# Norms moved beside matmuls in a two-block transformer forward: group norms, feed-forward norm, router weights, zero fill

## The chip, the cores and the metric

One core of a Trainium2 chip runs one program. The metric is the device time of one execution in microseconds (us), lower is better. Engines: TensorE (PE in the rows, its weight loads PEld), VectorE (DVE), ScalarE (ACT), GpSimd (POOL) and SyncE (SP), which here only issues DMAs and waits. A name with a q (SPq, PEq) is the engine's sequencer.

## The reference, cut to what matters

Two blocks of a network in fp32, on 512 tokens (and 256 context tokens in the first block) of width 1024. The change touches only the second block:

```
def second_block(x, ...):
    mod = silu(c) @ w_mod + b_mod             # six vectors: shift, scale, gate for mixer (m) and feed-forward (f)
    h = rms_norm(x, norm_mix) * (1 + scale_m) + shift_m
    proj = h @ w_in                           # 16 tiles of 128 columns (+ 4 columns for the forget gates)
    y_a = sliding_window_sink_attention(...)  # 512 columns, tiles 0..3
    y_b = rg_lru(conv(x_b)) * gelu(g_b)       # 256 columns, tiles 4, 5
    y_c = forgetting_attention(...)           # 256 columns, tiles 6, 7
    y = concat([rms_normalize(y_a), rms_normalize(y_b), rms_normalize(y_c)]) * out_gain
    x = x + gate_m * (y @ w_out)
    h = rms_norm(x, norm_ffn) * (1 + scale_f) + shift_f
    # router: 4 groups, 4 experts in each; best group by h @ w_rg, its best 2 experts by h @ w_re
    # each chosen expert: (silu(h @ w_gate[e]) * (h @ w_up[e])) @ w_down[e], weighted and summed
    x = x + gate_f * hierarchical_moe(h, ...)
    return rms_norm(x, norm_final)
```

## The kernel before, in words

**Layout.** Activations lie feature-major: `x` is [128, 8, 768], feature 128 k + p of a token in partition p of tile k. A matmul in near fp32 precision is three fp32r matmuls: every operand is split into a high part (rounded to fp32r, by ScalarE) and a low part (operand minus high part, by VectorE), and hi*hi, lo*hi and hi*lo are summed in PSUM (lines 912 to 914). Plain fp32 matmuls (the sums of squares against a matrix of ones, the transposes) take two passes each, and each pass is a record of its own.

**Blocks.** The program is a sequence of `nc.Block()`s. In a block each engine has a queue of its own, written out by hand in program order, tied by semaphores (`Tally`: a semaphore and the value it has reached). At a block's end all engines meet at a barrier. Semaphore waits stop the whole queue of the waiting engine.

**run_dense** (line 814) is the block for dense layers. A layer is cut into pieces of 128 output columns; each piece is one weight load of 512 KB on SP's queue (line 885) into one of two buffers, the split of the weights (ScalarE line 924, VectorE line 934), 24 matmuls of 512 columns (8 tiles times three) into one of two PSUM places, and the output by ScalarE or VectorE. The queue of ScalarE and of VectorE is, for piece n: split of piece n+1, then `behind` (a background program's step n), then the output of piece n. On TensorE step n of the background stands ahead of piece n. With `norm=` a norm runs in the same block: its sums come first, then the splits of pieces 0 and 1, then its apply part; TensorE waits tile by tile in piece 0 (`first_use`).

**Norms.** `normalize` (line 448) is a block of its own: squares on ScalarE (487), fp32 sums against ones on TensorE (476, in which two squares are ahead at most), variance on VectorE (525), Sqrt on ScalarE (489), reciprocal on VectorE (527), then per tile a multiplication (539) and gain on ScalarE (500), with `post` also high and low parts for the next matmuls (494, 547, 532). `Norm` is the same for use inside another block; in it POOL does the multiplication of the odd tiles (674) and VectorE that of the even ones, the high part is ScalarE's (614), the low part VectorE's (661, 665). With `xn=` the product goes to two scratch tiles, so POOL's tile k waits for the low part of tile k-2.

**The second block before.** (1) `run_dense` with the mixer's `Norm`, 16 pieces of `w_in_2` in the order `Branches.ORDER`, and `Branches` as background: convolution, LRU gates and scan, forget-gate cumulative sums, GELU, transposed values. Its last VectorE steps are those of n = 11 (1995 to 1999); the LRU's output is `xc`. POOL's program for the block (`Branches.pool`) ends with a memset and a DMA on POOL's queue, which writes zeros to all of `y_rows`, the experts' output rows in DRAM (2032 to 2034), and a wait for it. (2) `Branches.attend`: 24 units of two heads each through `Heads`; the output tiles end in `proj` 0 to 3 and 6, 7 (line 1314). SP does nothing there. (3) Three `normalize` blocks for y_a (4 tiles), y_b (2) and y_c (2), in place or into `proj`. (4) `run_dense` with the 8 pieces of `w_out_2`, ahead of which `split_before` splits all eight tiles of y (1064, 1069); TensorE waits for all eight. VectorE adds each piece to `x` (995). (5) `prenorm`: a `normalize` block for the feed-forward norm, 8 tiles, with `post`. (6) `experts`, one block to the end.

**experts.** SP loads the router's weights and some constants, then the experts' weights into five buffers of 1 MB (`e_raw`; a refill waits for the low part of the piece that lay there). The router has tokens as the stationary operand: for each of 4 groups of 128 tokens 8 x 3 matmuls with 20 moving columns (2394 to 2396). Then 64 matmuls against the identity turn h to token-major rows (2405, 2406), ScalarE copies them out (2501) and POOL stores them to DRAM (2353). VectorE meanwhile does some 60 small dependent instructions of the routing (2165 to 2231); in between TensorE sums the choices (2414, 2416). POOL scatters the slots (2357), reads them back, and gathers the rows of the first of 23 blocks of 128 tokens (2372), on which TensorE waits (2431). The blocks of experts follow, with a final norm at the end.

## Time and profile before

Three runs: 3625.29, 3631.13, 3632.75 us, median 3631.13. The profiled execution took 3634.53 us; its span from first to last instruction is 3632.5, mean granted TensorE clock 0.911 of 2.4 GHz.

| engine | busy us | share | instructions |
|---|---|---|---|
| PE | 3075.6 | 85% | 15929 |
| DVE | 1739.5 | 48% | 2638 |
| ACT | 1200.6 | 33% | 1833 |
| POOL | 488.1 | 13% | 419 |

DMA moved 338.73 MB, on average 93 GB/s. The second block takes the last 712 us of the span, from 2920 on. A timeline row reads: start in us from the span's start, duration (of a merged group: from its first start to its last end), engine, line, operation, output<-input, shapes, how many, and in brackets the idle time before it with what ended it. A row of `--windows` form gives a stretch, its length, busy time and count for PE, PEld, DVE, ACT and POOL, then granted clock, DMA share and GB/s.

### The profile page before, as it was taken

Reading aid. Unit: us, or ns where it says so; the run is one execution under the profiler, and the core shown is the slowest. Engines: PE = TensorE matmul, PEld = TensorE weight load, DVE = VectorE, ACT = ScalarE, POOL = GpSimd, SP = SyncE. Lnnn points to the kernel's source line nnn. Section 1 sums busy time; section 2 is a strip of 40 time slices with the busy share of each in tenths; the row PEclk is TensorE's granted clock in tenths of the full one; section 3 lists DMA queues with packets and bytes.
Section 4 is the critical chain, followed back from the end, with each engine's and each line's share of the span. In section 5 each row is a group of like instructions: output and inputs, shape, how many; then the busy total and the mean of one; then the engine's idle time right before and its main releaser. Section 6 shows DMA issues by size and latency. Waiting matters only on the chain. (4 is left out here: it accounts for less than half of the span.)

```text
span 3632.5 us, 39858 instructions
## 1 busy us (share of the span) xinstructions
PE 3075.6 (85%) x15929; PEld 2429.6 (67%) x15929; DVE 1739.5 (48%) x2638; ACT 1200.6 (33%) x1833; POOL 488.1 (13%) x419
## 2 busy tenths in 40 slices
PE   5579869799987999999698688997999977766995
PEld 3468545588875888888485456775878745346774
DVE  3664365422235554553512653335555352643886
ACT  4222344421113221221323453223222233522774
POOL 2240112200011000001311131001000003202222
PEclk8689989999997999999799899998999978885997
DMA  4774010122211443331440103322656226014971
GB/s 155 154 147 124 8 21 1 43 62 54 58 41 51 120 124 102 116 111 41 69 83 25 21 1 81 91 72 86 184 156 181 65 52 187 1 47 144 326 255 70
DMA packets 424353, 338.73 MB, mean 93 GB/s; under 512 B 38043, under 2 KB 372937, under 8 KB 424041
## 3 DMA queue, kind: packets, MB, share of 16 engines
...
## 5 line engine op out<-in xcount | busy, mean ns | idle before, releaser
L912 PE MATMUL ps<-ahi,w_hi 128*128 128x512 f32 (+1 forms) x2384 | 870.7, 365 | 171.6 <-DVE alo L665 84.0
L914 PE MATMUL ps<-alo,w_hi 128*128 128x512 f32 (+1 forms) x2384 | 858.2, 360 | 0.0
L913 PE MATMUL ps<-ahi,w_lo 128*128 128x512 f32 (+1 forms) x2384 | 857.9, 360 | 0.0
L912 PEld LDWEIGHTS ps<-ahi,w_hi 128*128 128x128 f32 x2384 | 462.0, 194 | 258.5 <-issue 60.0
L934 DVE TENSOR_TENSOR w_lo<-w_raw,w_hi 128x1024 fp32r<-128x1024 f32 (+2 forms) x248 | 359.8, 1452 | 445.0 <-ACT w_hi L924 444.2
L914 PEld LDWEIGHTS ps<-alo,w_hi 128*128 128x128 f32 x2384 | 461.5, 194 | 68.3
L913 PEld LDWEIGHTS ps<-ahi,w_lo 128*128 128x128 f32 x2384 | 462.6, 194 | 64.1
L924 ACT CAST w_hi<-w_raw 128x1024 fp32r<-128x1024 f32 (+2 forms) x248 | 289.5, 1169 | 507.4 <-PE ps L914 351.2
L746 DVE SCALAR_TENSOR_TENSOR vec_acc<-vec_w,csilu,vec_acc 128x512 f32<-128x512 f32 x364 | 263.0, 768 | 24.5 <-DMA vec_w<-in_w_mod 20.3
L1378 POOL TENSOR_SCALAR prob<-prob,nm 128x512 f32<-128x512 f32 (+4 forms) x104 | 163.8, 1575 | 717.8 <-DVE nm L1303 717.8
L1010 POOL TENSOR_TENSOR xsum<-x 128x768 f32<-128x768 f32 (+1 forms) x4 | 7.2, 1800 | 1485.9 <-DVE x L995 1485.9
L912 PE MATMUL ps<-hhi,w_hi 128*128 128x512 f32 (+1 forms) x528 | 190.6, 361 | 10.1 <-DVE hlo L1043 10.1
L995 DVE SCALAR_TENSOR_TENSOR x<-ps,mod,x 128x512 f32<-128x512 f32 x80 | 51.5, 669 | 289.4 <-PE ps L914 289.4
L913 PE MATMUL ps<-hhi,w_lo 128*128 128x512 f32 (+1 forms) x528 | 189.2, 358 | 0.0
L914 PE MATMUL ps<-hlo,w_hi 128*128 128x512 f32 (+1 forms) x528 | 188.7, 357 | 0.0
L1087 ACT ACTIVATE sg<-ps 128x768 f32<-128x768 f32 (+1 forms) x48 | 33.8, 705 | 425.4 <-PE ps L914 425.4
L1346 ACT ACTIVATE prob<-ps,nm 128x512 f32<-128x512 f32 (+4 forms) x208 | 140.4, 675 | 98.2 <-DVE nm L1296 58.4
L1248 PE MATMUL ps<-ident,prob 128*128 128x128 f32 x800 | 128.0, 290 | 30.9 <-ACT probT L1356 25.3
L1356 ACT COPY probT<-ps 128x384 f32<-128x384 f32 (+3 forms) x272 | 121.7, 477 | 81.2 <-PE ps L1248 81.1
L1095 DVE TENSOR_TENSOR gp<-sg,ps 128x768 f32<-128x768 f32 (+1 forms) x32 | 26.3, 821 | 244.0 <-ACT sg L1087 244.0
L2496 ACT CAST e_hi<-e_raw 128x2048 fp32r<-128x2048 f32 x69 | 131.5, 1911 | 29.4 <-DMA e_raw<-in_w_up 15.7
L1248 PEld LDWEIGHTS ps<-ident,prob 128*128 128x128 f32 x800 | 87.9, 145 | 76.8 <-issue 51.0
...
## 6 DMA issues: line engine op xcount, KB each, us to landing
vec_w<-in_w_mod SPq DMA_DIRECT2D x128, 512.0 KB, 4.2
...
```

What stands on the lines that cost most here:

```text
L746: m = dve.scalar_tensor_tensor(out=acc, in0=w, scalar=f, in1=acc, op0=ALU.mult, op1=ALU.add)
L912: pe.matmul(o, whi[:, j, b0 + b, :], hi[:, b, t0:t0 + tn], start=(b == 0), stop=False)
L913: pe.matmul(o, wlo[:, j, b0 + b, :], hi[:, b, t0:t0 + tn], start=False, stop=False)
L914: m = pe.matmul(o, whi[:, j, b0 + b, :], lo[:, b, t0:t0 + tn], start=False, stop=(b == nb - 1))
L924: act.copy(whi[:, j, 0:d.blocks, :], raw[:, j, 0:d.blocks, :]).then_inc(hi_ready[j].sem, 1)
L934: dve.tensor_tensor(wlo[:, j, 0:d.blocks, :], raw[:, j, 0:d.blocks, :], whi[:, j, 0:d.blocks, :].bitcast(F32), ALU.subtract).then_inc(lo_r ...
L995: m = dve.scalar_tensor_tensor(out=xo, in0=ps[:, b + t0:b + t0 + tn], scalar=mod[:, v, bass.ds(i * 2 + (gate + jj), 1)], in1=xo, op0=ALU.m ...
L1248: m = pe.transpose(ps[:, o:o + P], self.prob[:, j, n % self.bufs, (b0 + b) * P:(b0 + b + 1) * P], ident[:])
L1346: act.activation(self.prob[:, j, slot, 0:u.keys], self.scores_of(n, j), ACT.Exp, bias=nm[:, j, slot, 0:1], scale=self.sign, accum_out=nm[: ...
L1356: act.copy(self.probT[:, j, n % 2, b0 * P:(b0 + nb) * P], ps[:, o:o + nb * P]).then_inc(pt_done.sem, 1)
L1378: pool.tensor_scalar(self.prob[:, j, slot, 0:u.keys], self.prob[:, j, slot, 0:u.keys], self.nm[:, j, slot, 3:4], None, ALU.mult).then_inc( ...
L2496: act.copy(whi[:, n % HI, :], raw[:, n % RAW, :]).then_inc(e_hi.sem, 1)
```

## The change

- **Zero fill.** The memset and the DMA that writes zeros to `y_rows` leave `Branches.pool`. In the attention block POOL clears a tile of its own (`y_zero`) ahead of its work, and SP issues the DMA on its queue and waits for it there.
- **y_b.** Its norm is done by background steps in the input projection: squares on ScalarE at n = 12, two sums on TensorE ahead of piece 14, variance at n = 14, Sqrt, reciprocal and two multiplications in place at n = 15.
- **y_a and y_c.** A new class `GroupNorm` is the `norm=` of the output projection. It does six tiles of sums, two variances, two reciprocals; POOL multiplies tiles 1, 3 and 7, VectorE 0, 2 and 6. The gain is applied while the high and low parts are made, also for y_b, so `split_before` is gone.
- **Feed-forward norm.** `prenorm`'s block is gone. `experts` makes a `Norm` with scratch in `tok_major` and runs it inside its block, with the parts of each engine behind the first small steps of that engine.
- **Router.** The router's weights (20 columns) are the stationary operand and 512 tokens move: 8 x 3 matmuls, each tile's when its low part is there. ScalarE copies the [20, 512] logits to `lgT`, TensorE turns them in four transposes behind the first eight of the 64 row matmuls, and VectorE reads them from another bank.

```diff
+        class GroupNorm:
+
+
+            def __init__(self, c, proj, y_b, hi, lo):
+                self.y = [proj[:, k, :] for k in range(4)] + [y_b[:, k, :] for k in range(2)] + [proj[:, 6 + k, :] for k in range(2)]
+                self.hi, self.lo = hi, lo
+                self.sq = [sb(c, f"gr_sq{n}", [P, LAT])[:] for n in range(2)]
+                self.rstd = [sb(c, f"gr_rstd{n}", [P, LAT])[:] for n in range(2)]
+                self.stats = [(0, k) for k in range(4)] + [(1, k) for k in (6, 7)]
+
+                self.every = dict(zip((norm_sq, norm_var, norm_c, norm_sqrt, norm_rstd, *norm_x2, norm_hi, norm_lo), (6, 6, 2, 2, 2, 3, 3, KT, KT)))
+                self.c0 = {t: t.base for t in self.every}
+
+            def sem(self, t, n):
+                return t.sem, self.c0[t] + n
+
+            def total(self, gi):
+                return ps[:, BANK * (1 + gi):BANK * (2 + gi)]
+
+            def gain(self, k):
+                return col(vec3, V3_GAIN + k)
+
+            def act_stats(self, act):
+                for m, (gi, k) in enumerate(self.stats):
+                    if m >= 2:
+                        act.wait_ge(*self.sem(norm_var, m - 1))
+                    act.activation(self.sq[m % 2], self.y[k], ACT.Square).then_inc(norm_sq.sem, 1)
+
+            def pe(self, pe):
+                for m, (gi, k) in enumerate(self.stats):
+                    pe.wait_ge(*self.sem(norm_sq, m + 1))
+                    pe.matmul(self.total(gi), ones[:], self.sq[m % 2], start=(k in (0, 6)), stop=(k in (3, 7))).then_inc(norm_var.sem, 1)
+
+            def first_use(self, pe, k):
+                pe.wait_ge(*self.sem(norm_lo, k + 1))
+
+            def dve_stats(self, dve):
+                for gi, upto in ((0, 4), (1, 6)):
+                    dve.wait_ge(*self.sem(norm_var, upto))
+                    dve.tensor_scalar(self.rstd[gi], self.total(gi), 1.0 / (P * (4, 2)[gi]), RMS_EPS, ALU.mult, ALU.add).then_inc(norm_c.sem, 1)
+
+            def act_apply(self, act):
+                for gi in range(2):
+                    act.wait_ge(*self.sem(norm_c, gi + 1))
+                    act.activation(self.rstd[gi], self.rstd[gi], ACT.Sqrt).then_inc(norm_sqrt.sem, 1)
+                for k in range(KT):
+                    if k in (1, 3, 7):
+                        act.wait_ge(*self.sem(norm_x2[1], (k + 1) // 2 - (k == 7)))
+                    if k in (0, 2, 6):
+                        act.wait_ge(*self.sem(norm_x2[0], k // 2 + 1 - (k == 6)))
+                    act.activation(self.hi[:, k, :], self.y[k], ACT.Identity, scale=self.gain(k)).then_inc(norm_hi.sem, 1)
+
+            def dve_apply(self, dve):
+                def inverse(gi):
+                    dve.wait_ge(*self.sem(norm_sqrt, gi + 1))
+                    dve.reciprocal(self.rstd[gi], self.rstd[gi]).then_inc(norm_rstd.sem, 1)
+                    dve.wait_ge(*self.sem(norm_rstd, gi + 1))
+
+                def even(k, gi):
+                    dve.tensor_tensor(self.y[k], self.y[k], self.rstd[gi], ALU.mult).then_inc(norm_x2[0].sem, 1)
+
+                def low(k):
+                    dve.wait_ge(*self.sem(norm_hi, k + 1))
+                    dve.scalar_tensor_tensor(out=self.lo[:, k, :], in0=self.y[k], scalar=self.gain(k), in1=self.hi[:, k, :].bitcast(F32),
+                                             op0=ALU.mult, op1=ALU.subtract).then_inc(norm_lo.sem, 1)
+
+                inverse(0)
+                even(0, 0)
+                even(2, 0)
+                low(0)
+                low(1)
+                inverse(1)
+                even(6, 1)
+                for k in range(2, KT):
+                    low(k)
+
+            def pool(self, pool):
+                for m, (k, gi) in enumerate(((1, 0), (3, 0), (7, 1))):
+                    pool.wait_ge(*self.sem(norm_rstd, gi + 1))
+                    pool.tensor_tensor(self.y[k], self.y[k], self.rstd[gi], ALU.mult).then_inc(norm_x2[1].sem, 1)
+
+            def ended(self):
+                for t, n in self.every.items():
+                    t.base += n
...
+                if n == 14:
+                    pe.wait_ge(yb_square.sem, 2)
+                    for k in range(2):
+                        m = pe.matmul(ps[:, 6 * BANK:6 * BANK + LAT], ones[:], self.tmp[:, k, :], start=(k == 0), stop=(k == 1))
+                    m.then_inc(yb_sum.sem, 1)
...
+                    act.wait_ge(yb_done.sem, 1)
+                    for k in range(2):
+                        act.activation(self.tmp[:, k, :], self.xc[:, k, :], ACT.Square).then_inc(yb_square.sem, 1)
+                if n == 15:
+                    act.wait_ge(yb_var.sem, 1)
+                    act.activation(self.r[:, 0, :], self.r[:, 0, :], ACT.Sqrt).then_inc(yb_root.sem, 1)
...
-                    ch.mark(dve.tensor_tensor(self.xc[:], self.xc[:], self.r[:], ALU.mult))
+                    dve.tensor_tensor(self.xc[:], self.xc[:], self.r[:], ALU.mult).then_inc(yb_done.sem, 1)
                     dve.wait_ge(swa_in.sem, 32)
                     ch.mark(dve.tensor_scalar(self.nsinks[:], self.sinks[:], -1.0, None, ALU.mult))
+                if n == 14:
+                    dve.wait_ge(yb_done.sem, 1)
+                    dve.wait_ge(yb_sum.sem, 1)
+                    dve.tensor_scalar(self.r[:, 0, :], ps[:, 6 * BANK:6 * BANK + LAT], 1.0 / LRU_W, RMS_EPS, ALU.mult, ALU.add).then_inc(yb_var.sem, 1)
+                if n == 15:
+                    dve.wait_ge(yb_root.sem, 1)
+                    ch.link(dve.reciprocal(self.r[:, 0, :], self.r[:, 0, :]))
+                    for k in range(2):
+                        ch.mark(dve.tensor_tensor(self.xc[:, k, :], self.xc[:, k, :], self.r[:, 0, :], ALU.mult))
...
-                zero = self.ck[:, 0:2, :].rearrange("p a n -> p (a n)")
-                pool.memset(zero, 0.0).then_inc(pool_chain.sem, 1)
-                pool.wait_ge(pool_chain.sem, p + 1)
-                pool.dma_start(y_rows[:].rearrange("(r b) d -> r b d", b=N_BLOCKS), zero.unsqueeze(1).to_broadcast([P, N_BLOCKS, D])).then_inc(y_zeroed.sem, 16)
-                pool.wait_ge(y_zeroed.sem, 16)
...
-                attend(Heads(c, units))
+                zero = sb(c, "y_zero", [P, D])
+                z0 = pool_chain.base + 1
+
+                def cleared(pool):
+                    pool.memset(zero[:], 0.0).then_inc(pool_chain.sem, 1)
+
+                def fill(sp):
+                    sp.wait_ge(pool_chain.sem, z0)
+                    sp.dma_start(y_rows[:].rearrange("(r b) d -> r b d", b=N_BLOCKS), zero[:].unsqueeze(1).to_broadcast([P, N_BLOCKS, D])).then_inc(y_zeroed.sem, 16)
+                    sp.wait_ge(y_zeroed.sem, 16)
+
+                attend(Heads(c, units, before={"pool": cleared}), fill)
+                pool_chain.base += 1
...
+            spare = tm[:].rearrange("p t d -> p (t d)").rearrange("p (n m) -> p n m", m=LAT)
+            norm = Norm(c, xt(LAT), LAT, RMS_EPS, lambda k: col(vec1, V_FFN + k), (ahi, alo, *modulate_by(mod, 3)),
+                        [spare[:, 0, :], spare[:, 1, :]], spare[:, 2, :], [spare[:, 3, :], spare[:, 4, :]], xn=[spare[:, 5, :], spare[:, 6, :]])
+            lgT = spare[0:NG + N_EXP, 7, :]
...
+                norm.dve_stats(dve)
...
+                norm.dve_apply(dve)
                 dve.wait_ge(ld[1].sem, ld[1].base + 48)
-                dve.wait_ge(pe_chain.sem, pc + 1)
+                dve.wait_ge(t_done.sem, t_done.base + 1)
                 NR = NG + N_EXP
-                ch.link(dve.tensor_tensor(logits[:], ps[:, 7 * BANK:7 * BANK + 4 * NR].rearrange("p (t n) -> p t n", n=NR),
+                ch.link(dve.tensor_tensor(logits[:], ps[:, 5 * BANK:5 * BANK + 4 * NR].rearrange("p (t n) -> p t n", n=NR),
...
+                norm.pool(pool)
...
+                norm.pe(pe)
                 pe.wait_ge(dve_chain.sem, dc + 1)
-                for t in range(4):
-                    tok = slice(t * P, (t + 1) * P)
-                    o = ps[:, 7 * BANK + t * NR:7 * BANK + (t + 1) * NR]
-                    for k in range(KT):
-                        pe.matmul(o, ahi[:, k, tok], nw_hi[:, k, :], start=(k == 0), stop=False)
-                        pe.matmul(o, alo[:, k, tok], nw_hi[:, k, :], start=False, stop=False)
-                        m = pe.matmul(o, ahi[:, k, tok], nw_lo[:, k, :], start=False, stop=(k == KT - 1))
-                m.then_inc(pe_chain.sem, 1)
-                pe.wait_ge(act_chain.sem, ac + 2)
-                for u in range(8):
+                o = ps[0:NR, 7 * BANK:7 * BANK + LAT]
+                for k in range(KT):
+                    norm.first_use(pe, k)
+                    pe.matmul(o, nw_hi[:, k, :], ahi[:, k, :], start=(k == 0), stop=False)
+                    pe.matmul(o, nw_hi[:, k, :], alo[:, k, :], start=False, stop=False)
+                    m = pe.matmul(o, nw_lo[:, k, :], ahi[:, k, :], start=False, stop=(k == KT - 1))
+                m.then_inc(prep_mm.sem, 1)
+
+                def rows_of_h(u):
                     t, half = u // 2, u % 2
                     if u >= 4:
                         pe.wait_ge(tok_major.sem, u - 3)
@@ -2405,6 +2525,15 @@
                         pe.matmul(o, ahi[:, 4 * half + k, t * P:(t + 1) * P], ident_r[:], start=True, stop=False)
                         m = pe.matmul(o, alo[:, 4 * half + k, t * P:(t + 1) * P], ident_r[:], start=False, stop=True)
                     m.then_inc(x_turned.sem, 1)
+
+                pe.wait_ge(act_chain.sem, ac + 2)
+                rows_of_h(0)
+                pe.wait_ge(prep_act.sem, prep_act.base + 1)
+                for t in range(4):
+                    m = pe.transpose(ps[:, 5 * BANK + t * NR:5 * BANK + (t + 1) * NR], lgT[:, t * P:(t + 1) * P], ident[0:NR, 0:NR])
+                m.then_inc(t_done.sem, 1)
+                for u in range(1, 8):
+                    rows_of_h(u)
...
+                norm.act_stats(act)
+                norm.act_apply(act)
+                act.wait_ge(prep_mm.sem, prep_mm.base + 1)
+                act.copy(lgT, ps[0:NG + N_EXP, 7 * BANK:7 * BANK + LAT]).then_inc(prep_act.sem, 1)
...
-                def prenorm(v, s):
-                    with ExitStack() as c1:
-                        h = sb(c1, "h", [P, KT, LAT])
-                        normalize([h[:, k, :] for k in range(KT)], LAT, RMS_EPS, lambda k: col(vec1, v + k), post=(ahi, alo, *modulate_by(mod, s)), src=xt(LAT))
...
-                    for first, n in ((0, 4), (4, 2), (6, 2)):
-                        normalize([proj[:, first + k, :] for k in range(n)], LAT, RMS_EPS, lambda k: col(vec3, V3_GAIN + first + k),
-                                  src=[branches.xc[:, k, :] for k in range(2)] if first == 4 else None)
                     with ExitStack() as c2:
-                        run_dense(new_ring(c2, KT), [residual(mod, g["w_out_2"][0], 2 * KT, KT, (ahi, alo), LAT, adds={y_hi: KT, y_ready: KT},
-                                                              before=split_before(proj, 0, ahi, alo, KT, LAT))])
-                prenorm(V_FFN, 3)
+                        run_dense(new_ring(c2, KT), [residual(mod, g["w_out_2"][0], 2 * KT, KT, (ahi, alo), LAT)],
+                                  norm=GroupNorm(c2, proj, branches.xc, ahi, alo))
                 experts(c, ahi, alo, mod)
```

## Rows read from the trace of the kernel before

**Rows 1.** Busy times of the router's stretch (PE, PEld, DVE, ACT, POOL, clock, DMA, GB/s).
```profile
3278.00:3302.00 24.00, 20.53 (x97) 20.53 (x97) 1.58 (x13) 0.52 (x2) 2.54 (x3) 0.50 0.92 290
```

**Rows 2.** Timeline around the zero fill: start us, duration, engine, instruction, idle before.
```profile
3043.11 1.51 POOL L2034 DMA_DIRECT2D y_rows<-fox_ck  x1 [0.30 <-POOL fox_ck L2032]
3063.20 1.04 ACT L924 CAST w_hi<-w_raw 128x1024 fp32r<-128x1024 f32 x1 [7.80 <-DMA w_raw<-in_w_in]
3065.55 0.79 PE L912 MATMUL ps<-a2hi,w_hi 128*128 128x512 f32 x1 [5.19 <-DVE w_lo L934]
3086.95 0.60 ACT L970 ACTIVATE proj<-ps 128x512 f32<-128x512 f32 x1 [9.22 <-PE ps L914]
3087.86 0.93 PE L1235 MATMUL ps<-swa_k,proj 64*128 64x128 f32 x8 [0.94 <-PEq L867]
```

**Rows 3.** DMA view, 3000 to 3300 us: kilobytes, then us to landing.
```profile
y_rows<-fox_ck POOLq DMA_DIRECT2D x1, 11776.0 KB, 37.1
```

**Rows 4.** Weight buffer, landing times from 3040 to 3095, then 3010 to 3042 us.
```profile
DMA to landing us min/median/max: 6.5/16.8/25.5
DMA to landing us min/median/max: 5.7/6.4/6.5
```

**Rows 5.** Timeline at the first group norm.
```profile
3154.09 0.69 DVE L1314 COPY proj<-ps 128x512 f32<-128x512 f32 x1 [4.26 <-PE ps L1259]
3155.76 3.83 PE L476 MATMUL ps<-sq,ones 128*128 128x512 f32 x8 [1.72 <-ACT sq L487]
3158.43 1.28 ACT L489 ACT_TABLE_LOAD   x1
3161.02 3.35 DVE L527 RECIPROCAL rstd<-rstd 128x512 f32<-128x512 f32 x1 [0.69 <-ACT rstd L489]
```

**Rows 6.** Timeline of the output projection: first matmul, clock's rise, first and last update.
```profile
3202.67 0.79 PE L912 MATMUL ps<-a2hi,w_hi 128*128 128x512 f32 x1 [18.36 <-DVE a2lo L1069]
3206.68 0.55 PE L912 MATMUL ps<-a2hi,w_hi 128*128 128x512 f32 x1
3210.53 0.75 DVE L995 SCALAR_TENSOR_TENSOR x<-ps,mod,x 128x512 f32<-128x512 f32 x1 [6.78 <-PE ps L914]
3249.74 0.75 DVE L995 SCALAR_TENSOR_TENSOR x<-ps,mod,x 128x512 f32<-128x512 f32 x1 [4.85 <-PE ps L914]
```

**Rows 7.** Timeline of the mixer's norm beside its first projection tile.
```profile
2920.33 1.15 ACT L605 ACTIVATE sq<-x 128x512 f32<-128x512 f32 x2 [0.28 <-PEq L456]
2921.01 10.40 PE L592 MATMUL ps<-sq,ones 128*128 128x512 f32 x16 [12.75 <-ACT sq L605]
2933.87 0.68 DVE L646 TENSOR_SCALAR rstd<-ps 128x512 f32<-128x512 f32 x1
2938.68 1.77 POOL L674 TENSOR_TENSOR xn<-x,rstd 128x512 f32<-128x512 f32 x1 [48.02 <-DVE rstd L648]
2943.97 1.58 DVE L665 TENSOR_TENSOR a2lo<-tmp,a2hi 128x512 fp32r<-128x512 f32 x1
2954.11 0.69 DVE L665 TENSOR_TENSOR a2lo<-tmp,a2hi 128x512 fp32r<-128x512 f32 x1
2956.56 0.59 ACT L970 COPY proj<-ps 128x512 f32<-128x512 f32 x1 [2.61 <-PE ps L914]
```

**Rows 8.** Timeline, experts' block up to the routing.
```profile
3277.78 0.37 SPq L2297 DMA_DIRECT2D nw<-in_w_router_group  x1
3280.74 0.32 ACT L2508 CAST nw_hi<-nw 128x160 fp32r<-128x160 f32 x1 [3.64 <-DMA nw<-in_w_router_expert]
3301.98 0.45 PE L2405 MATMUL ps<-ident_r,a2hi 128*128 128x128 f32 x1
3308.19 0.23 DVE L2184 TENSOR_TENSOR route_both<-route_chosen 128x64 f32<-128x64 f32 x1
3315.67 4.39 PE L2414 MATMUL ps<-route_both,e_upto 128*128 128x17 f32 x20
3321.87 0.29 DVE L2199 TENSOR_TENSOR route_masked<-route_chosen,ps 128x128 f32<-128x128 f32 x1 [7.59 <-PE ps L2416]
```

5 lines of the change are left out of this document (3 added, 2 removed).

## The prediction, made before the changed kernel ran

> **What bounds the kernel now.** I read the code's order first, then the table of stretches from 3040 to 3350 us, then the timeline at each border, then the waits of the weight buffer. The program is a chain of blocks with a barrier of all engines at each end, so the chain of waits on the page begins only where the last block starts, 3277.8 us, and says nothing of the part that changes; the borders have to be read from the timeline. Four places matter.
>
> End of the input projection: 16 pieces of 24 matmuls go at 5.60 us each. The zero fill, 11,776 KB, is issued by POOL at 3043.11 and needs 37.1 us [rows 2, 3]. Weight loads issued meanwhile land after up to 25.5 us, against 5.7 to 6.5 before [rows 4]. ScalarE stands 7.80 us for a load and TensorE 5.19 us for its split; the first attention matmul is at 3087.86 [rows 2]. Group norms: attention's last copy ends at 3154.78 [rows 5] and the output projection's first matmul is at 3202.67 [rows 6], 47.9 us of three short blocks and a split in which TensorE has almost nothing. Feed-forward norm: from 3250.8, a barrier's 0.3 behind the last update's end at 3250.49 [rows 6], until the next block at 3277.78 [rows 8], TensorE again nearly empty. Router: 96 matmuls of 20 columns at half clock, 20.53 us of the stretch at 0.50 [rows 1]; the 64 transposing matmuls follow from 3301.98 to 3315.67, and the routing waited 7.59 us for what TensorE does behind them [rows 8]. So in these stages each dependent step counts in full.
>
> **Part 1, zero fill to the attention stage, LRU norm into the projection's end.** TensorE would finish piece 13 at 3065.55 - 5.19 = 3060.36 with or without the fill. Without it the loads are back at 6 us, which a piece of 5.60 us and two buffers cover (they did until 3043). Added ahead of piece 14: two fp32 sums, four passes. Eight passes took 3.83 us [rows 5], so 1.9 us; they wait for two squares that ScalarE does three pieces earlier. Everything behind them on TensorE waits too: 3060.36 + 1.9 + 2 x 5.60 = 3073.5. Then the tail on ScalarE and VectorE: Sqrt comes after ScalarE's copy of piece 14 at 3068.5, with a table load of 1.28 [rows 5] and about 0.63, so 3070.4; reciprocal 3.35 [rows 5], 3073.8; two multiplications at 0.65 to 0.69 [rows 7], 3075.1. The last copy of ScalarE is done at 3074.1, so VectorE is late last, by 1.0 us. The barrier took 3087.86 - 3087.55 = 0.3 [rows 2]: attention starts at 3075.4 instead of 3087.86, 12.5 us less. Exp's table must now be loaded again at its start; ScalarE stood there 0.9 us anyway, so 0.4 is lost. I take 12.1. Bounds: a loss of 4 (if the loads were late for another reason, the added 1.9 + 1.0 + 0.4 and slack remain), and 14.5 (sums hidden).
>
> The fill itself: POOL's memset, then one DMA on SP's queue, where nothing else is queued in that block; attention runs 3087.86 to 3154.78, 66.9 us, and the fill took 37.1. It costs nothing as long as it takes under about 65 us. No row shows this transfer on SP's queue; that queue moved 290 GB/s in 3278 to 3302 [rows 1], at which it would take 41.
>
> The Trainium skill (ScalarE: Activation LUTs, "What ACT_TABLE_LOAD costs") puts a table switch at 1.28 us and a drain of 1.38 behind it. The load in this trace is 1.28 [rows 5], and the activations that follow such loads start at once or when their operand comes. By the page the two added switches would cost up to 2.8 us more; I go by the row.
>
> **Part 2, group norms beside the output projection.** Before: 3154.78 to the end of the last update, 3249.74 + 0.75 = 3250.49 [rows 5, 6]. After, from the same point: ScalarE starts squares at 3155.1. Four tiles of sums took until 3155.76 + 3.83 = 3159.59, two per 1.85, so six until 3161.4. Weights were loaded meanwhile. ScalarE: two high halves at 1.04 [rows 2] until 3162.4, table 1.28, Sqrt, 3164.3. VectorE: two variances, then two low halves at 1.3 at most (3064.24 to 3065.55 [rows 2]) until 3164.7, reciprocal 3.35: 3168.1. Now POOL multiplies tiles 1 and 3 at 1.77 us [rows 7], VectorE tiles 0 and 2 and the low parts 0 and 1. Do they overlap? In the same kind of norm VectorE's subtraction took 1.58 instead of 0.69 when a multiplication of POOL ran [rows 7]: it stood until POOL had done. So I let them exclude each other where both want to go: low part 1 at 3172.5, second reciprocal until 3175.9, POOL's tile 7 until 3177.7, then six low parts at 0.69, the first at 3178.4. If they overlapped freely this would be 1.9 earlier. TensorE does tiles 0 and 1 alone, then six groups of three matmuls, at half clock 1.28 a group (3202.67 to 3206.68 holds nine matmuls and the clock rises there, after 4.0 us [rows 6]): three groups until 3182.4, the rest at 0.70: piece 0 is done at 3184.4. Updates come every (3249.74 - 3210.53) / 7 = 5.60 us [rows 6]: the last ends at 3184.5 + 39.2 + 0.75 = 3224.5. Gain 26.0; bounds 23.5 (the clock rises a piece's rest later, more exclusion) and 28 (free overlap).
>
> The Trainium skill (SBUF — State Buffer, "Who interferes with whom") says that a VectorE instruction with two SBUF inputs and a GpSimd instruction that reads SBUF exclude each other for the whole instruction. That speaks against giving three tiles to POOL, and the 1.58 above [rows 7] agrees; by the rule the sum is the 26.0, without it 27.9.
>
> **Part 3, feed-forward norm in the experts' block, weights of the router stationary.** Before: 3250.8 to the first transposing matmul, 3301.98 [rows 8]. After: the block starts at 3250.8, but ScalarE first waits for the router's weights: its first cast was 2.96 after that block's start (3277.78 to 3280.74 [rows 8]) and with two casts the squares start 3.5 late, 3254.3. This is a cost that the old order did not have. From there I take the mixer's norm, the same class with the same two scratch tiles, POOL on odd tiles, and TensorE cold: from the first square at 2920.33 to the last low part at 2954.11 + 0.69 = 2954.80 [rows 7]. In it VectorE did two weight splits before the variance: sums done at 2921.01 + 10.40 = 2931.41, variance at 2933.87, so 2.4 don't recur. 34.5 - 2.4 = 32.1: last low part at 3286.4. TensorE follows with three matmuls per tile, 24 instead of 96, and is 1.7 behind at the end (2954.80 to 2956.56 [rows 7]): 3288.1. The copy of the logits (some 0.6) lies beside the first eight transposing matmuls. Their four transposes are eight passes at 4.39 / 20 = 0.22 [rows 8]: 1.75. The 64 transposing matmuls stay. TensorE is thus done with them 3301.98 - 3288.1 - 1.75 = 12.1 us earlier. The routing gets its logits at 3291.6 and needs some 6.4 us to the table that TensorE multiplies (3301.98 to 3308.42 [rows 8]), 3298.0, while TensorE is at 3303.5: TensorE stays late last, the 7.59 [rows 8] shrinks little. Bounds: 9 (the norm 3 slower) and 15 (TensorE still at full clock for the sums: its gap of about 5 us is like the 5.19 after which it was at half [rows 2]).
>
> What is behind hangs on the same points: the five weight buffers of the experts fill ahead of need in both versions, and the next loads wait for VectorE, which comes out of the routing. So the 282 us behind 3350 move as a whole, at no cost.
>
> **Sum.** 12.1 + 26.0 + 12.1 = 50.2. The profiled execution took 3634.53 (span 3632.5 and 2.0 around it), so 3584.3 in its terms; it was 3.4 above the median, 3631.13, in whose terms the forecast is 3581.
>
> **Rivals.** A, *the clock rises behind the router*. The new router's 24 matmuls stream 512 columns back to back at its end, after which the mixer's clock had risen; the transposing matmuls might then run at 0.11 instead of 0.213. Against: with 64 of them in a row the clock never rose before. TensorE would be done before the routing, which would then be last at 3298.0 (5.5 less), and the 28 small matmuls behind, 3315.67 to 3321.87, would halve: about 8.5 more, 3572.5. B, *the fill was not what starved the projection*. For it: loads were 6 us, not 4, already before. Against: 25.5 right under the fill. Part 1 is then -4, total 34: 3597. C, *the group norm's two reciprocals and POOL hold TensorE longer*, with a cold clock through piece 0 and again in the norm behind: parts 2 and 3 give 23 and 7, total 42: 3589. D, *the fill on SP's queue is slow*: attention's barrier waits for it. It decides from 65 us on, and makes the kernel slower from 65 + 50 = 115 us, under 105 GB/s; at 80 GB/s it would take 147 us, 82 over: 3581 + 82 = 3663. Against: 290 GB/s on that queue [rows 1].
>
> **How the numbers follow.** Forecast 0.60, A 0.15, C 0.14, B 0.07, D 0.04. The forecast's own range is 3575 to 3587, from the parts' bounds; A and C on its sides and part of B give 3569 to 3595. A measurement tells 0.2%, 7 us, from no change. Faster by that: all but D, 0.95; within: 0.02 (a D of 110 to 120 us); slower: 0.03.
>
> **What would show it.** Part 1: in the last two pieces no wait of ScalarE on its weights; attention starts near 3075; a table load at its start; the fill lands inside attention. Part 2: 3154.78's counterpart to the last update about 70 us instead of 96, subtractions of about 1.5 us on VectorE beside POOL. Part 3: squares 3.5 us into the block, 24 router matmuls spread over the low parts, 64 transposing ones at 0.213. Wrong would be: a wait of all engines on SP at attention's end, stages behind 3350 that do not shift rigidly, or a clock of 1.0 under the transposing matmuls.

## The result and the profile after

The changed kernel takes 3585.9 us (median of 4 runs, 3578.1 to 3597.8) beside 3631.9 for the kernel before on the same chip (4 runs, 3625.3 to 3641.7): 0.9874 of it, 95% interval [0.9834, 0.9913]. Run again with the experiments it gave 3581.5, 0.9852 [0.9824, 0.9880]. The forecast was 3581. The profiled execution took 3578.06 (span 3576.3), 56.5 less than the profiled one before.

A single execution can lie 8 us off either way: the code ahead of the change is the same in every kernel here, and yet ScalarE copied piece 12 of the input projection as early as 3048.2 and as late as 3065.0 us. So I compare stretches between six borders that each trace has: that copy; attention's first matmul; the end of attention's last copy; the start of the output projection's last update; TensorE's first transpose of gathered tokens; the end of the span. All are differences of timeline rows, in us. In the labels, serial means in a block of its own, and dummies are matmuls that nothing reads.

| kernel | piece 12 at | to attention | attention | to last update | to gather | to end |
|---|---|---|---|---|---|---|
| before | 3054.80 | 33.06 | 66.92 | 94.96 | 99.74 | 283.02 |
| changed | 3052.77 | 20.49 | 66.75 | 69.29 | 85.28 | 281.72 |
| changed, again (e9) | 3060.81 | 20.49 | 66.89 | 69.42 | 85.09 | 281.80 |
| e1 fill on POOL | 3059.45 | 31.63 | 62.58 | 69.24 | 85.25 | 283.75 |
| e2 group norms serial | 3055.05 | 20.50 | 66.91 | 83.78 | 85.35 | 281.41 |
| e3 ffn norm serial | 3059.32 | 20.48 | 66.70 | 69.30 | 78.02 | 284.88 |
| e4 squares first | 3064.81 | 20.49 | 66.92 | 69.43 | 79.71 | 280.34 |
| e5 squares first, hold | 3063.10 | 20.49 | 66.97 | 69.34 | 76.49 | 280.51 |
| e6 squares first, dummies | 3053.85 | 20.49 | 62.52 | 69.46 | 71.61 | 281.67 |
| e7 group norms on VectorE | 3048.20 | 20.49 | 65.45 | 69.24 | 75.67 | 283.45 |
| e8 dummies in group norms | 3050.64 | 20.48 | 62.66 | 68.93 | 74.97 | 281.82 |
| e10 combined | 3052.18 | 20.49 | 62.49 | 66.20 | 71.95 | 281.49 |
| e11 combined, more dummies | 3064.99 | 20.49 | 65.58 | 67.78 | 73.05 | 283.01 |
| e12 ffn serial, new order | 3060.32 | 20.49 | 66.98 | 66.20 | 78.31 | 284.20 |

Of the 56.2 us between the two spans, 2.0 were there before the change begins and 1.3 come behind the gather, neither more than the same code moves from run to run. The change itself brings 12.6 in the projection's end, 0.2 in attention, 25.7 with the group norms and 14.5 with the feed-forward norm and the router: 52.9.

The timeline of the changed kernel at the projection's end and attention's start is the counterpart of [rows 2]; columns are start us, duration, engine, line, instruction, and idle time before it:

```profile
3065.68 0.60 ACT L1056 ACTIVATE proj<-ps 128x512 f32<-128x512 f32 x1 [5.78 <-PE ps L1000]
3066.30 1.28 ACT L2024 ACT_TABLE_LOAD   x1
3067.59 0.63 ACT L2024 ACTIVATE lru_r<-lru_r 128x512 f32<-128x512 f32 x1
3068.26 3.35 DVE L2103 RECIPROCAL lru_r<-lru_r 128x512 f32<-128x512 f32 x1 [6.49 <-ACT lru_r L2024]
3071.28 0.60 ACT L1056 ACTIVATE proj<-ps 128x512 f32<-128x512 f32 x1 [3.06 <-PE ps L1000]
3071.64 1.29 DVE L2105 TENSOR_TENSOR lru_x<-lru_x,lru_r 128x512 f32<-128x512 f32 x2
3073.22 1.28 ACT L1431 ACT_TABLE_LOAD   x1 [1.34 <-PEq L953]
3073.26 0.93 PE L1321 MATMUL ps<-swa_k,proj 64*128 64x128 f32 x8 [2.01 <-PEq L953]
3074.19 0.61 SPq L2176 DMA_DIRECT2D y_rows<-y_zero  x1
3074.51 0.29 ACT L1431 ACTIVATE sink_e<-swa_sinks,nm 128x1 f32<-128x1 f32 x1
```

The last two copies are 5.60 us apart and neither waits for a DMA. The copies of pieces 13 and 14 start at 3058.38 and 3065.68, 7.30 apart, since y_b's two sums stand between these pieces on TensorE. VectorE's chain on y_b ends at 3072.93, 1.05 behind ScalarE's last copy, and lets the block end. The fill goes out within attention; the DMA view from 3060 to 3120 us gives its kilobytes and the us to landing:

```profile
y_rows<-y_zero SPq DMA_DIRECT2D x1, 11776.0 KB, 33.1
```

From the timeline of the changed kernel around the output projection's first piece, VectorE, POOL and TensorE (the counterpart of [rows 5, 6]):

```profile
3139.32 0.69 DVE L1400 COPY proj<-ps 128x512 f32<-128x512 f32 x1 [5.72 <-PE ps L1345]
...
3155.04 1.71 POOL L761 TENSOR_TENSOR proj<-proj,gr_rstd 128x512 f32<-128x512 f32 x1
3155.54 2.41 DVE L745 SCALAR_TENSOR_TENSOR a2lo<-proj,vec,a2hi 128x512 fp32r<-128x512 f32 x2
3157.44 0.77 PE L998 MATMUL ps<-a2hi,w_hi 128*128 128x512 f32 x1 [10.48 <-DVE a2lo L745]
3157.88 3.34 DVE L737 RECIPROCAL gr_rstd<-gr_rstd 128x512 f32<-128x512 f32 x1
3163.67 0.79 PE L998 MATMUL ps<-a2hi,w_hi 128*128 128x512 f32 x1 [3.33 <-DVE a2lo L745]
3170.11 0.75 DVE L1081 SCALAR_TENSOR_TENSOR x<-ps,mod,x 128x512 f32<-128x512 f32 x1 [3.17 <-PE ps L1000]
...
3209.30 0.75 DVE L1081 SCALAR_TENSOR_TENSOR x<-ps,mod,x 128x512 f32<-128x512 f32 x1 [4.85 <-PE ps L1000]
```

TensorE waits twice: 10.48 us for the first low part and 3.33 for tile 2's, which stands behind the second reciprocal. Two low parts take 2.41 beside POOL. The experts' block (timeline, the counterpart of [rows 8]):

```profile
3213.72 0.32 ACT L2637 CAST nw_hi<-nw 128x160 fp32r<-128x160 f32 x1 [14.50 <-DMA nw<-in_w_router_expert]
3214.15 1.14 ACT L606 ACTIVATE tok_major<-x 128x512 f32<-128x512 f32 x2
3214.83 9.53 PE L593 MATMUL ps<-tok_major,ones 128*128 128x512 f32 x16 [5.56 <-ACT tok_major L606]
3246.68 0.31 PE L2525 MATMUL ps<-ident_r,a2hi 128*128 128x128 f32 x1
3248.41 0.61 PE L2533 MATMUL ps<-ident,tok_major 20*128 20x20 f32 x4
3249.13 0.24 DVE L2284 TENSOR_TENSOR logits<-ps,route_b 128x80 f32<-128x80 f32 x1 [3.80 <-PE ps L2533]
```

The first square waits for the cast, as forecast. Table of stretches of the same trace (busy us of PE, PEld, DVE, ACT, POOL with counts, then granted clock, DMA share, GB/s):

```profile
3233.00:3245.00 12.00, 8.87 (x20) 1.74 (x18) 11.27 (x16) 4.59 (x6) 5.13 (x4) 0.50 0.18 70
3252.00:3254.00 2.00, 2.00 (x11) 2.00 (x11) 1.69 (x10) 1.32 (x2) 0.39 (x1) 0.50 0.53 217
3268.00:3270.00 2.00, 2.00 (x11) 2.00 (x11) 1.79 (x12) 0.00 (x0) 0.00 (x0) 0.50 0.00 0
3270.00:3272.00 2.00, 2.00 (x19) 2.00 (x18) 1.76 (x16) 0.90 (x2) 0.00 (x0) 0.91 0.01 4
```

From 3233 to 3245 the router's matmuls run at the norm's pace, at 1.2 GHz (0.50). From 3246 TensorE is busy without a gap, with the 64 row matmuls and then smaller ones, and still stays at 1.2 GHz until about 3270. The experiments on the feed-forward norm turn on these rows.

### The profile page after: what moved, and what is told of

Its sections match the earlier page's. It is cut to its first block and busy times, and to the rows that moved or that the text cites. A ratio compares the mean times of both kernels' runs of the same rounds, so it can differ in the third digit from the quotient of the medians.

```text
span 3576.3 us, 39662 instructions
## 1 busy us (share of the span) xinstructions
PE 3056.3 (85%) x15861; PEld 2406.6 (67%) x15861; DVE 1741.2 (49%) x2631; ACT 1194.6 (33%) x1820; POOL 495.1 (14%) x425
## 3 DMA queue, kind: packets, MB, share of 16 engines
q1 hardware_dynamic: 409384, 307.15, 30.1%
```

## The experiments

Diffs are against the changed kernel; three dots stand for lines not shown. "Last update to gather" is the fifth column of numbers in the table above.

**e1: the fill back on POOL's queue in the input projection.**

```diff
+                zero = self.ck[:, 0:2, :].rearrange("p a n -> p (a n)")
+                pool.memset(zero, 0.0).then_inc(pool_chain.sem, 1)
+                pool.wait_ge(pool_chain.sem, p + 1)
+                pool.dma_start(y_rows[:].rearrange("(r b) d -> r b d", b=N_BLOCKS), zero.unsqueeze(1).to_broadcast([P, N_BLOCKS, D])).then_inc(y_zeroed.sem, 16)
+                pool.wait_ge(y_zeroed.sem, 16)
...
-                attend(Heads(c, units, before={"pool": cleared}), fill)
+                attend(Heads(c, units))
```

> The changed kernel with one thing undone: the zero fill of y_rows is issued on POOL's queue at the end of the input projection again, as in the kernel before; the norm of y_b stays at the projection's end. Theory: the fill is what starves the projection's last weight loads, so the wait of about 20 us for piece 14 (landing of w_raw up to 25 us) returns, and the attention stage starts about 12 us later than in the changed kernel: 3598 us beside 3586, and the norm of y_b costs nothing there, since it lies in the wait. Rival: the weights come late for another reason (the order of SP's queue) and the 12 us came from the norm of y_b alone: then the time stays within 2 us of the changed kernel and the loads land in 6 to 7 us in spite of the fill.

Measured: 3593.4 us, 0.9892 [0.9863, 0.9921]. The stretch to attention is 31.63 instead of 20.49. ScalarE's timeline shows the two waits:

```profile
3067.42 1.04 ACT L1010 CAST w_hi<-w_raw 128x1024 fp32r<-128x1024 f32 x1 [7.37 <-DMA w_raw<-in_w_in]
3080.37 1.04 ACT L1010 CAST w_hi<-w_raw 128x1024 fp32r<-128x1024 f32 x1 [11.41 <-DMA w_raw<-in_w_in]
```

Rows of the weight buffer from 3040 to 3092 us, first of e1 and then of the changed kernel (shortest, median and longest time from issue to landing):

```profile
DMA to landing us min/median/max: 6.1/17.6/25.0
```

```profile
DMA to landing us min/median/max: 6.5/6.9/7.3
```

The fill starved the projection; that is shown. Taking it out gives 11.1 us (31.63 - 20.49). Beside the fill y_b's norm costs nothing (31.63 with it, 33.06 in the kernel before without it). No run takes y_b's norm out where the fill is gone, but the rows of the changed kernel show its price there: the 7.30 us between two copies instead of 5.60, and VectorE 1.05 late at the end. In the profiled execution 4.2 us of this were given back, since attention took 62.58 instead of 66.75; that is no effect of the fill, as e6, e8 and e10 have 62.5 to 62.7 with the fill in attention. The stretches of 30 us inside attention, first e1 and then the changed kernel:

```profile
3111.00:3141.00 30.00, 25.00 (x209) 14.87 (x208) 23.39 (x112) 22.85 (x97) 12.38 (x14) 1.00 0.01 2
```

```profile
3093.00:3123.00 30.00, 25.97 (x172) 14.64 (x173) 20.91 (x100) 19.70 (x85) 10.26 (x12) 0.83 0.41 165
```

In one the clock holds, in the other it falls for some microseconds; the kernel before had 0.83 as well, with a DMA share of 0.01.

**e2: group norms ahead of the output projection, in blocks of their own** (y_b still normalized in the input projection).

```diff
+                    for first, n in ((0, 4), (6, 2)):
+                        normalize([proj[:, first + k, :] for k in range(n)], LAT, RMS_EPS, lambda k: col(vec3, V3_GAIN + first + k))
...
                     with ExitStack() as c2:
-                        run_dense(new_ring(c2, KT), [residual(mod, g["w_out_2"][0], 2 * KT, KT, (ahi, alo), LAT)],
-                                  norm=GroupNorm(c2, proj, branches.xc, ahi, alo))
+                        run_dense(new_ring(c2, KT), [residual(mod, g["w_out_2"][0], 2 * KT, KT, (ahi, alo), LAT, adds={y_hi: KT, y_ready: KT},
+                                                              before={"act": split_act, "dve": split_dve, "pe": lambda pe: pe.wait_ge(y_ready.sem, y_ready.base + KT)})])
```

`split_act` and `split_dve` (not shown) make the high and low parts of all eight tiles ahead of the projection.

> The changed kernel with the group norms taken out of the output projection again: two norms of groups 0 and 2 in blocks of their own, then the split and the projection; y_b is still normalized at the end of the input projection. Theory: what the second part gains is the serial chain of group norms and of the split, without the y_b block, so the stretch from the end of attention to the last update is 70 us plus what two of the three blocks and the split cost. In the kernel before the three norms took about 39 us of the 95.7, some 9 to 10 of them for y_b; so the stretch should be 84 to 87 us, the time about 3601 us. Rival: the overlap itself brings nothing because VectorE's and POOL's shared work sets TensorE's pace; then the stretch stays within 4 us of 70.

Measured: 3593.4 us, 0.9893 [0.9865, 0.9921]; to the last update 83.78 instead of 69.29. So the second part's 25.7 us are 14.5 from the overlap and 11.2 (94.96 - 83.78) from y_b's block, which the first part had made needless.

**e3: feed-forward norm in its own block, 24 router matmuls kept.**

```diff
-                norm.pe(pe)
                 pe.wait_ge(dve_chain.sem, dc + 1)
...
+                    normalize([h[:, k, :] for k in range(KT)], LAT, RMS_EPS, lambda k: col(vec1, V_FFN + k), post=(ahi, alo, *modulate_by(mod, 3)), src=xt(LAT))
                 experts(c, ahi, alo, mod)
```

> The changed kernel with the feed-forward norm in a block of its own ahead of the experts again; the router keeps its weights stationary (24 matmuls of 512 columns, transposes of the logits). Theory: the overlap hides the router's matmuls and the loads and casts behind the norm; serial, the norm's block takes about 31 us, then block entry, casts and the 24 matmuls (24 x 0.6 at half clock = 14 us, or 24 x 0.3 = 7 at full) run after it, so the stretch from the norm's first square to the routing's first sum grows by 8 to 14 us: 3594 to 3600 us. Rival: the gain of this part came from the 24 matmuls in place of 96 alone and the overlap is worth nothing: then within 2 us of the changed kernel.

Measured: 3580.7 us, 0.9851 [0.9825, 0.9877]. Neither theory: the gather comes 7.3 us *earlier* than in the changed kernel (78.02 against 85.28), although the logits come 1.4 later (41.23 against 39.83 behind the last update). The difference lies behind the logits. Timeline of TensorE in e3:

```profile
3251.81 0.63 PE L2508 MATMUL ps<-a2lo,nw_hi 128*20 128x512 f32 x1
3252.24 0.63 PE L2509 MATMUL ps<-a2hi,nw_lo 128*20 128x512 f32 x1
3252.66 0.53 PE L2507 MATMUL ps<-a2hi,nw_hi 128*20 128x512 f32 x1
3253.03 0.40 PE L2508 MATMUL ps<-a2lo,nw_hi 128*20 128x512 f32 x1
3253.26 0.40 PE L2509 MATMUL ps<-a2hi,nw_lo 128*20 128x512 f32 x1
```

and the stretch behind the router:

```profile
3256.00:3266.00 10.00, 10.00 (x91) 9.82 (x89) 6.30 (x40) 8.29 (x14) 2.14 (x4) 1.00 1.09 362
```

The 24 matmuls run without gaps here, the clock rises 5 us into them, and the 64 row matmuls behind start every 0.11 us instead of every 0.21. In the changed kernel the 24 come three at a time at the norm's pace and the clock stays at half. Against the kernel before, the router's new form with the norm still serial brings 21.7 us (99.74 - 78.02): 12.5 at the first row matmul (52.24 to 39.77 behind the last update), the rest behind it, where the clock is now high. In these two profiles the overlap gives 7.3 of them back. The medians can't confirm that difference, 3580.7 here and 3581.5 for the changed kernel run again.

**e4: squares ahead of the casts.** Base of e5 and e6.

```diff
+                norm.act_stats(act)
                 act.wait_ge(ld[0].sem, ld[0].base + 32)
                 act.copy(nw_hi[:], nw[:]).then_inc(act_chain.sem, 1)
                 act.copy(ident_r[:], ident[:]).then_inc(act_chain.sem, 1)
-                norm.act_stats(act)
```

> The changed kernel with one move on ScalarE in the experts' block: the squares of the feed-forward norm are issued ahead of the two casts of the router weights and of the identity, which wait for a DMA. Theory: the casts hold the first square back by 3.5 us, and the whole chain down to the routing starts at that square, so the time falls by about 3.5 us, to 3582 us (with the squares 0.5 us after the block's start). The casts then come 13 us later, still ahead of the first router matmul. Rival: the norm's first use is set by the weights' low part, which VectorE makes after the cast and ahead of its reciprocal in order; then the cast, now behind the squares, delays VectorE's variance by its own length and the gain falls to 1 to 2 us, or below nothing.

Measured: 3575.8 us, 0.9834 [0.9810, 0.9858]; the gather 79.71 behind the last update, 5.6 earlier than in the changed kernel. More than 3.5, because TensorE comes to the sums sooner behind the projection and does them at full clock:

```profile
3223.38 7.52 PE L593 MATMUL ps<-tok_major,ones 128*128 128x512 f32 x16 [1.77 <-ACT tok_major L606]
```

In the changed kernel the same group took 9.53.

**e5: e4, and TensorE waits for the last low part ahead of the router.**

```diff
+                norm.first_use(pe, KT - 1)
                 for k in range(KT):
                     norm.first_use(pe, k)
```

> Squares ahead of the casts, and TensorE waits in the experts' block for the last low part of the normed state before it starts the router's 24 matmuls, so that these run without gaps. All stretches from the last update of the output projection. With the norm serial, the logits came at 41.2 us and the gather's first transpose at 78.0, and the clock rose 5 us into the gapless matmuls, so that the 64 matmuls for the rows took 0.11 us each; with the norm beside the router (squares first) 34.5 and 79.7, with the clock at half and 0.21 us each. Theory (the clock, which the norm's pace keeps low, is what the overlap costs): the last low part is there at 30.7; 12 matmuls at 0.43 and 12 at 0.23, then the transposes: logits at about 40, gather at 77, 3 us earlier than with squares first alone in spite of the later start. Rival (the gather comes early in the serial form because loads or POOL's queue stand better there, not the clock): the logits come 5.5 us later and so does the gather, 85.

Measured: 3574.8 us, 0.9835 [0.9808, 0.9862]; logits at 39.13, gather at 76.49. The first router matmul starts 13.2 us later than in e4 (30.77 instead of 17.61 behind the last update) and the logits come 4.6 later, and yet the gather comes 3.2 earlier. That speaks for the clock and against the rival. The stretches of e5 show the clock rising among the 24, about 3 us into them:

```profile
3250.00:3252.00 2.00, 1.33 (x4) 0.54 (x5) 0.57 (x1) 0.00 (x0) 0.00 (x0) 0.50 0.02 7
3252.00:3256.00 4.00, 4.00 (x16) 1.57 (x15) 0.00 (x0) 0.00 (x0) 0.00 (x0) 0.79 0.00 0
3256.00:3260.00 4.00, 4.00 (x30) 3.06 (x29) 0.83 (x5) 1.16 (x2) 0.00 (x0) 1.00 0.00 0
```

**e6: e4, and matmuls that nothing reads while TensorE waits for the norm.**

```diff
                 for k in range(KT):
+                    for _ in range(1 if k else 7):
+                        pe.matmul(warm_bank, ones[:], x[:, 0, 0:LAT], start=True, stop=True)
                     norm.first_use(pe, k)
```

> Squares ahead of the casts, and matmuls that nothing reads on TensorE while it waits for the feed-forward norm: seven fp32 ones of 512 columns (0.95 us each at full clock, 1.9 at half) ahead of the first router group, one ahead of each later group. They go into an unused bank; the result is unchanged. Stretches from the last update of the output projection; squares first alone: logits at 34.5 us, gather's first transpose at 79.7. Theory (the clock is what the overlap costs): the clock stays high through the router, the logits come at 33 to 35, the 64 matmuls for the rows take 0.11 us each, and the gather follows the logits by 37 instead of 45: 71 us, the time 8.5 us below squares first, about 3567 to 3570. Rival: the idle gaps between the norm's steps bring the clock down all the same; then each dummy takes 1.9 us, each group 3.2 instead of 1.9, the logits come at about 45 and the gather at 85 to 90.

Measured: 3562.2 us, 0.9816 [0.9787, 0.9844]; logits at 33.25, gather at 71.61, 8.1 earlier than in e4. The router's stretches of e6 all stand at full clock:

```profile
3226.00:3236.00 10.00, 8.51 (x26) 2.90 (x25) 9.48 (x13) 3.98 (x5) 4.86 (x4) 1.00 0.69 237
3236.00:3246.00 10.00, 10.00 (x78) 8.67 (x76) 6.47 (x38) 6.06 (x13) 1.60 (x3) 1.00 0.21 82
```

**e7: all group multiplications on VectorE.**

```diff
-                even(0, 0)
-                even(2, 0)
+                for k in range(4):
+                    even(k, 0)
...
                 even(6, 1)
+                even(7, 1)
...
-                    pool.tensor_tensor(self.y[k], self.y[k], self.rstd[gi], ALU.mult).then_inc(norm_x2[1].sem, 1)
+                pass
```

> The changed kernel with all six multiplications of the group norms on VectorE, none on POOL. Stretch from the end of attention to the last update: 70.0 us in the changed kernel, 69.3 to the last update's start. There a VectorE multiplication beside POOL's takes 1.19 us, alone 0.66. Theory (POOL's help costs as much as it brings): multiplications 2.6 instead of 2.4 us ahead of the first low parts, the low parts 1.3 instead of 2.4, the second reciprocal 1 us earlier, the third low part at about 22.3 instead of 24 us: the stretch 1 to 1.5 us shorter. Rival (TensorE and its clock set the stretch, not VectorE's order): the clock rises when it did, and the stretch stays within 0.4 us.

Measured: 3580.5 us, 0.9863 [0.9841, 0.9885]; to the last update 69.24, no change. By the length alone that would be the rival, but two effects cancel here. VectorE is faster without POOL: two low parts take 1.41 us instead of 2.41, and from the start of the first variance to the end of the last low part it needs 20.50 us instead of 21.78, 1.3 less, as the theory had it. But in this execution the clock fell during the six sums ahead of the variance. Their row in the changed kernel, then their row and their first 4 us in e7:

```profile
3141.29 5.68 PE L713 MATMUL ps<-gr_sq,ones 128*128 128x512 f32 x12 [2.02 <-ACT gr_sq L708]
```

```profile
3135.41 7.29 PE L713 MATMUL ps<-gr_sq,ones 128*128 128x512 f32 x12 [2.01 <-ACT gr_sq L708]
3135.00:3139.00 4.00, 3.58 (x5) 1.61 (x6) 0.00 (x0) 1.51 (x3) 0.00 (x0) 0.57 0.88 242
```

So everything behind the sums started 1.6 us later. The same fall in e11 made the same stretch 1.6 us longer than in e10. One profile at one clock level thus does not decide between theory and rival by its length; the rows inside it give the theory's 1.3 us.

**e8: dummies in the group norms.**

```diff
             def first_use(self, pe, k):
+                for _ in range({0: 8, 2: 2}.get(k, 0)):
+                    pe.matmul(ps[:, 3 * BANK:3 * BANK + LAT], ones[:], x[:, 0, 0:LAT], start=True, stop=True)
```

> The changed kernel with matmuls that nothing reads on TensorE while it waits for the group norms: eight fp32 ones of 512 columns ahead of the output projection's first group and two ahead of its third. Stretch from the end of attention to the last update's start: 69.3 us. Theory (the first piece runs at half clock: 17 of its 24 matmuls at 0.43 instead of 0.23 us, 3.4 us): the first piece then ends as soon as the last low part is there, 1.5 to 2.5 us earlier, and so do all updates. Rival: the dummies run at half clock (1.9 us each, 15 for eight) and hold the first group back: 2 to 6 us longer.

Measured: 3574.3 us, 0.9851 [0.9818, 0.9883]; to the last update 68.93, only 0.4 less. The first tiles ran at full clock, then TensorE stood 2.94 us for the third tile all the same: for that tile VectorE's order is the bound, not the clock. Behind it the clock fell once more (0.50 from 3158.7 to 3162.0), so this run does not show what a high clock through the whole first piece would give.

Both e7 and e8 show something unasked: their experts' block is that of the changed kernel, and yet the gather came at 75.67 and 74.97. So I ran the changed kernel once more.

**e9: the changed kernel itself.**

> The changed kernel itself once more, for a second profile. In its first profile the clock stayed at half through the router and the 64 matmuls for the rows, and the gather's first transpose came 85.3 us after the last update of the output projection; two kernels with the same experts' block (all group multiplications on VectorE; dummies in the group norms) came at 75.7 and 75.0 with the clock risen. Theory (whether the clock rises there changes from one execution to the next of the same code): this profile shows either about 75 or about 85, and the attention stage 62.6 or 66.8 us likewise. Rival (the two kernels' earlier first update or shorter group norms set it): 85 again.

Measured: 3581.5 us; gather at 85.09. With e1 and e2, whose experts' block is the same too, four profiles show 85.1 to 85.4 and two 75.0 and 75.7. In e7 the clock rose while the norm still paced the router:

```profile
3234.00:3236.00 2.00, 1.12 (x4) 0.22 (x3) 1.92 (x3) 1.32 (x2) 0.31 (x1) 0.93 0.00 0
```

So the form of the changed kernel leaves the clock open. Whether the shorter time of e7 and e8 has a cause in their group norms is not settled by one profile each. The rows differ in little: in the four the clock fell for the last time 19.3 to 20.4 us behind the last update and then stayed low, in the two at 20.7 and 20.8 and then rose again.

**e12: the serial form again, with a new order of the group norms.** (Run after e10 and e11.) The order, also in e10 and e11, where as in e7 POOL multiplies nothing; e3's edit is in e12 too:

```diff
-                low(0)
-                low(1)
+                for k in range(6):
+                    low(k)
                 inverse(1)
                 even(6, 1)
-                for k in range(2, KT):
+                even(7, 1)
+                for k in range(6, KT):
                     low(k)
```

> The changed kernel with the feed-forward norm in a block of its own again (24 router matmuls kept), and with all group multiplications on VectorE, low parts 0 to 5 ahead of the second reciprocal. A second profile of the serial form, and the new order of the group norms without any dummies. Theory for the serial form (the router's matmuls run without gaps behind a stretch of idling, so the clock rises 5 us into them every time): last update to the gather's first transpose 78.0 us again, against 85.3 and 85.1 in the two profiles of the changed kernel. Rival (the clock rises there in some executions and not in others whatever the form, as in the two kernels that came at 75.7 and 75.0): about 85 here, or within 1 us of 78 by chance. For the order: end of attention to the first update 27.0 to 28.6 us as in the two kernels with that order, instead of 30.1.

Measured: 3574.4 us, 0.9827 [0.9789, 0.9866]; gather at 78.31 (e3: 78.02), last update at 66.20 instead of 69.3. The serial form came to 78 both times. Of the 3.1 us at the first update (27.00 instead of 30.10), the last low part brings 1.0 (25.91 instead of 26.92 behind attention's end); the other 2.1 come because only six of the piece's 24 matmuls are left behind the second reciprocal, not 18, and because these run at full clock (0.50 until 21.3 us behind attention's end instead of 28.0).

**e10: squares first, dummies, and that order.** Diff: those of e4 and e6 and the order of e12 together.

> Squares ahead of the casts, matmuls that nothing reads while TensorE waits for the feed-forward norm, and all group multiplications on VectorE with the low parts that need no second reciprocal (0 to 5) ahead of it. Theory: last update of the output projection to the gather's first transpose 71.6 us as with the dummies before; end of attention to the first update 29 us instead of 30.1, since only six matmuls are left behind the last low parts (the last of them at 22 us, then 1.4 to 2.5 us of matmuls). Time about 3560 to 3565. Rival for the new order: the last low part comes 0.5 us later than before, and the first update with it: 30.5 us.

Measured: 3564.2 us (5 runs), 0.9808 [0.9785, 0.9830], beside 3581.5 for the changed kernel on the same chip. End of attention to the first update: 27.0 us instead of 30.1, where 29 were expected. VectorE's timeline of e10:

```profile
3148.40 2.50 DVE L739 TENSOR_TENSOR proj<-proj,gr_rstd 128x512 f32<-128x512 f32 x4
3150.81 2.74 DVE L743 SCALAR_TENSOR_TENSOR a2lo<-proj,vec,a2hi 128x512 fp32r<-128x512 f32 x4
3153.46 1.41 DVE L743 SCALAR_TENSOR_TENSOR a2lo<-lru_x,vec,a2hi 128x512 fp32r<-128x512 f32 x2
3154.79 3.35 DVE L735 RECIPROCAL gr_rstd<-gr_rstd 128x512 f32<-128x512 f32 x1
3162.16 0.75 DVE L1078 SCALAR_TENSOR_TENSOR x<-ps,mod,x 128x512 f32<-128x512 f32 x1 [1.10 <-PE ps L997]
```

TensorE now has six tiles' work while the second reciprocal runs. With e6 and e11 this is the fastest version; the intervals of the three overlap, and e10's also touches those of e4, e5 and e12, so the times alone do not rank them.

**e11: e10 and 14 more dummies ahead of the gather's first transpose.**

```diff
+                for _ in range(14):
+                    pe.matmul(ps[:, 7 * BANK:7 * BANK + LAT], ones[:], x[:, 0, 0:LAT], start=True, stop=True)
                 pe.wait_ge(tok_major.sem, 18)
                 turn(0)
```

> The kernel above and 14 further fp32 matmuls that nothing reads ahead of the gather's first transpose, where TensorE has nothing to do for 19 us. Theory: the clock is then high when the experts' first gate and up matmuls start (at half clock 12 of them take 0.43 us each and more follow, from 5 us after the start at 0.23), so the stage from the first transpose to the end is 2 to 3.5 us shorter: 278 instead of 281.5 us. Rival: weights, not TensorE, are the bound of the first experts, or the clock falls within the last idle microseconds before the gather: no change beyond 1 us.

Measured: 3564.4 us, 0.9804 [0.9781, 0.9827]; to the end 283.01 against 281.49. The theory's 278 did not come, and the run is inconclusive on its cause: the dummies were over 8.06 us before the gathered rows came, and the experts' first matmuls still ran at half clock. In this execution the clock also fell in the sums of the group norms (to the last update 67.78 instead of 66.20, same code).

## Why the prediction was right

The forecast's three terms, 12.1, 26.0 and 12.1, sum to 50.2; measured in the profiled execution they are 12.6, 25.7 and 14.5.

*Part 1* held step by step. In the terms of the kernel before (plus 2.03, the offset at piece 12) attention starts at 3075.3, forecast 3075.4; VectorE is late last by 1.05 us, forecast 1.0; the first sink activation comes 14.29 - 2.03 = 12.3 us earlier (3088.80 before, 3074.51 now), forecast 12.1. Both added table loads took 1.28 us, and the activation behind each started 1.29 after the load's start, so the row, not a longer switch, was the right price. Rival B is refuted by e1. Rival D too: the fill landed after 33.1 us, under the 37.1 of [rows 3].

*Part 2*: 70.0 us from the end of attention to that of the last update, forecast 69.7. Low part 1 was done at 17.9 us (17.7) and the second reciprocal at 21.2 (21.1), so the wait of VectorE beside POOL was sized about rightly; the first update came at 30.1 us (29.7). What the working did not say is that y_b's block alone was 11.2 of the 26 (e2), and that the wait behind the second reciprocal (3.33) could be shortened by order: e10 and e12 end the first piece 3.1 us earlier.

*Part 3* is the term that was mis-sized, 12.1 where 14.5 were measured. TensorE starts the row matmuls 37.37 us behind the last update instead of 52.24, 14.9 earlier, where the working has 3301.98 - 3288.1 = 13.9. Of that 1.0 the sums of squares gave 0.9: the working took 10.40 us for them from [rows 7], with about 6 us of them at half clock, and they took 9.53, since the clock was at half only until 3219.2, 4.4 us of them. (The first square was 3.8 us late, forecast 3.5.) Another 1.1 is in the four transposes, 0.61 us instead of the 1.75 taken from the small matmuls of [rows 8]. The 64 row matmuls at half clock were forecast rightly for this execution, and there some luck was in it, as rival A shows.

*Rival A* deserved more than 0.15. Its mechanism is real: in e7 and e8 the same experts' block was through 9.6 and 10.3 us earlier with the clock up, where 8.5 were forecast. The argument against it, "with 64 of them in a row the clock never rose before", is true as far as it goes: in the six profiles in which the 64 began at half clock (before, changed, e9, e1, e2, e4) they took 13.9 to 14.5 us each time and it did not rise under them. What it left out is that the clock can be high when they begin, as in the other eight, where they took 7.75. The clock that the router's matmuls leave behind is what decides. The prediction treated the overlap of norm and router as pure cover. Its price was a clock that the gapped matmuls left at half: the norm in its own block (e3, e12) is 7 us *faster* to the gather than the overlap in four of the six profiles with the changed kernel's experts' block and up to 3 slower in two. The gain of part 3 comes from the router's new form; the overlap paid in each of its profiles only where the gaps were filled (71.6 in e6, 72.0 in e10, 73.1 in e11, squares first in all three, against 78.0 and 78.3 for the serial form).

*Rival C*: two reciprocals and POOL held TensorE 0.4 us longer than reckoned, not 3. POOL's share does cost something, the 1.3 us on VectorE that e7's rows show.

The remaining difference, 46.0 us between medians against 52.9 in the traces, lies within the scatter of the runs (interval [0.9834, 0.9913]: 32 to 60 us).
